# An opening that scales its rows first and adds their shift last

## What is computed

```python
mod = cond @ ada_w[l] + ada_b[l]                 # cond = silu(c)
sh1, sc1, g1, sh2, sc2, g2 = jnp.split(mod, 6, axis=-1)
h = modulate(rms_norm(x, norm_mix_g[l]), sh1, sc1)      # h * (1 + scale) + shift
proj = h @ w_in                                  # layer 0: q, k, v of two kinds of attention
# stick-breaking attention (8 heads) and sliding-window attention (8 heads), then
x = x + g1 * (o @ w_out)
h = modulate(rms_norm(x, norm_ffn_g[l]), sh2, sc2)
x = x + g2 * conv_ffn(h, ...)
# layer 1: the same around an HGRN2 recurrence; a last rms_norm closes
```

## Time and profile before

| | |
|---|---|
| Median of 3 runs | 1299.79 us (1299.79 to 1300.24) |
| Profiled execution, its own time | 1300.57 us |
| Span of the profiled execution | 1298.8 us |
| Mean granted TensorE clock | 0.997 |
| TensorE busy | 97% of the span |
| VectorE busy | 63% |
| ScalarE busy | 43% |
| GpSimd busy | 4% |

### The profile page before, as it was taken

One profiled execution on the slowest core, in us unless ns is written; L12 is line 12 of the kernel. 1 busy time (PEld: TensorE's weight loads), 2 busy tenths in 40 slices (PEclk: granted clock), 3 DMA queues, 4 the chain that ended last, 5 costly groups with the idle time before them and its releaser, 6 DMA issues.

```text
span 1298.8 us, 18991 instructions
## 1 busy us (share of the span) xinstructions
PE 1262.1 (97%) x7071; PEld 1021.7 (79%) x7071; DVE 818.4 (63%) x1191; ACT 554.8 (43%) x837; POOL 46.8 (4%) x92
## 2 busy tenths in 40 slices
PE   6999998999999999999999999999999999999997
PEld 5777777868888888878778888888688888888786
DVE  5776667676666666556787887776855555552423
ACT  7665556343333333121356655653433333331212
POOL 1000000000000000001000000001000000000000
PEclk9999999999999999999999999999999999999999
DMA  9644520535445454556513222226233333332232
GB/s 331 196 130 146 163 81 2 163 97 162 145 142 146 134 154 145 172 160 226 184 55 94 66 82 74 78 78 210 66 102 96 96 95 97 97 97 97 92 103 81
DMA packets 190074, 160.09 MB, mean 123 GB/s; under 512 B 5271, under 2 KB 163176, under 8 KB 190018
## 3 DMA queue, kind: packets, MB, share of 16 engines
q1 hardware_dynamic: 177696, 116.34, 29.7%
q0 software_dynamic: 11776, 42.29, 10.8%
q10 hardware_dynamic: 546, 0.69, 0.1%
HBM read 157.20 MB, written 2.10 MB: 123 GB/s over the span
## 4 chain that ended last, share of the span: by engine, by line
PE 88%; DVE 5%; SPq 2%; ACT 2%; issue 1%; DMA 1%; DVEq 0%; ACTq 0%
PE proj L1684 62%; PE z L1684 21%; PE obank L1684 3%; PE misc L1684 1%; SPq L512 1%; SPq L522 1%; DVE normed L1106 1%; DVE hT_lo L1112 1%; ACT w_hi L654 1%; DMA w_raw<-ab_w_in 1%; DVE w_lo L1068 0%; DVE xT L1491 0%; PE z L2244 0%; ACT hT_hi L686 0%; PE misc L1957 0%
## 5 line engine op out<-in xcount | busy, mean ns | idle before, releaser
L1684 PE MATMUL proj<-hT_hi,w_hi 128*128 128x512 f32 x1112 | 439.6, 396 | 1.1 <-ACT hT_hi L686 0.9
L1684 PE MATMUL proj<-hT_lo,w_hi 128*128 128x512 f32 x1112 | 434.6, 391 | 2.9 <-DVE hT_lo L1112 2.9
L1068 DVE TENSOR_TENSOR w_lo<-w_raw,w_hi 128x1024 fp32r<-128x1024 f32 x189 | 231.1, 1224 | 321.4 <-ACT w_hi L654 321.3
L1684 PE MATMUL proj<-hT_hi,w_lo 128*128 128x512 f32 x1112 | 433.2, 390 | 0.0
L654 ACT ACTIVATE w_hi<-w_raw 128x1024 fp32r<-128x1024 f32 x191 | 201.9, 1058 | 404.0 <-PE proj L1684 230.9
L1684 PEld LDWEIGHTS proj<-hT_lo,w_hi 128*128 128x128 f32 x1112 | 208.8, 188 | 52.4 <-DVE hT_lo L1112 9.3
L1684 PEld LDWEIGHTS proj<-hT_hi,w_hi 128*128 128x128 f32 x1112 | 208.8, 188 | 50.3 <-issue 8.7
L1684 PEld LDWEIGHTS proj<-hT_hi,w_lo 128*128 128x128 f32 x1112 | 208.7, 188 | 44.2
L1684 PE MATMUL z<-gated_hi,w_hi 128*128 (+1 forms) x264 | 103.6, 392 | 2.7 <-DVE xT L1491 2.7
L1684 PE MATMUL z<-gated_hi,w_lo 128*128 (+1 forms) x264 | 103.1, 390 | 0.0
L1684 PE MATMUL z<-gated_lo,w_hi 128*128 (+1 forms) x264 | 103.0, 390 | 0.0
(11 more groups left out here) (342 smaller groups left out, 1485.5 us busy)
## 6 DMA issues: line engine op xcount, KB each, us to landing
ada_raw<-ada_w POOLq DMA_DIRECT2D x80, 512.0 KB, 4.2
w_raw<-ffn_w_gate SPq DMA_DIRECT2D x44, 512.0 KB, 3.8
w_raw<-ffn_w_up SPq DMA_DIRECT2D x44, 512.0 KB, 3.8
w_raw<-ffn_w_down SPq DMA_DIRECT2D x44, 512.0 KB, 3.3
w_raw<-hg_w_in SPq DMA_DIRECT2D x32, 512.0 KB, 4.1
ada_first<-ada_w SPq DMA_DIRECT2D x16, 512.0 KB, 11.0
w_raw<-ab_w_in SPq DMA_DIRECT2D x14, 512.0 KB, 4.0
w_raw<-ab_w_out SPq DMA_DIRECT2D x8, 512.0 KB, 4.2
```

The lines of the kernel that those rows point to most:

```text
L1068: nc.vector.tensor_tensor(w_lo[:, slot, :], w_raw[:, slot, :], w_hi[:, slot, :].bitcast(F32), ALU.subtract).then_inc(lo_done, 1)
L1684: return nc.tensor.matmul(dst, weights_ap, moving, start=start, stop=stop, skip_group_check=True)
```

## The change

- The loads are cut anew: weights of four units in four pieces of two channel blocks each (`quad_load`), between them the scale weights in three pieces of 2, 2 and 4 blocks (`SCALES`), and last the shift weights. Two further units (`EARLY`) are loaded among the shift pieces.
- x is turned unscaled. The factor of each row is spread by TensorE over all partitions (`diag`, two banks), and `x_hat` = xT times that row, made by VectorE for blocks 0 and 1 and by GpSimd for blocks 2 to 7 (`hat`). VectorE copies blocks 0 to 3 of xT out of the banks, ScalarE the rest.
- The first two pieces of scale columns are made by TensorE alone, in small products of the raw weights with cond (`scale_products`); the third as before, by sums on VectorE.
- The blocks `hT_hi` and `hT_lo` carry the scale but not the shift. The four units, now SQ, SQ+1, SK, SK+1, run over these. Their missing part, the weights times the shift, is a column of each unit (`quad_bias_of`, 128 small products behind the shift sums) that is added when the units are copied out of the banks.
- Then the blocks are made again with the shift (`shifted_high` on ScalarE, `shifted_value` and `shifted_low` on VectorE), for all later units; the first of them (SV) waits for them one by one (`fix_lo`).
- GpSimd also makes three of the four low parts of these units' weights (`quad_split`) and those of the next two units (`early_split`).
- SV and WK become ordinary units, both ahead of "B" 0; "T" 0 goes behind it.

```diff
-QUAD = [SQ, SK, SV, WK]
+QUAD = [SQ, SQ + 1, SK, SK + 1]
 STEPS0 = [
-    ("Q", 0), ("A", 0), ("T", 0), ("u", SQ + 1), ("B", 0), ("u", SK + 1),
+    ("Q", 0), ("A", 0), ("u", SV), ("u", WK), ("B", 0), ("T", 0),
...
+EARLY = len(QUAD) + 2
+PIECES = 4
+SCALES = [(0, 2, 0), (1, 2, 2), (2, 4, 4)]
+X_BASE = 4
...
             quad_load(0)
-            first_ada(1)
+            scale_load(0)
             quad_load(1)
+            scale_load(1)
+            quad_load(2)
+            scale_load(2)
+            quad_load(3)
+            sp.wait_ge(xt_full, DC)
+            for k in range(4):
+                shift_load(k)
+            unit_load(4)
             sp.dma_start(table2, tables[:, 2 * P:9 * P]).then_inc(bands_in, 16)
-            for u in range(4, len(UNITS0)):
-                if u < 6:
-                    sp.wait_ge(quad_low, u - 1)
+            for k in range(4, DC):
+                shift_load(k)
+            unit_load(5)
...
+            def hat(dc):
+                if dc < X_BASE:
+                    pool.wait_ge(x_early, dc + 1)
+                else:
+                    pool.wait_ge(x_new, dc + 1 - X_BASE)
+                nc.gpsimd.tensor_tensor(x_hat(dc), xT[:, dc, :], x_rstd[:], ALU.mult).then_inc(hat_pool, 1)
+            def quad_split(c):
+                pool.wait_ge(hi_done, c + 1)
+                if c == 2:
+                    pool.wait_ge(misc_full, MISC_AT["scale1"] + 1)
+                nc.gpsimd.tensor_tensor(quad_lo[c], quad_raw[c], quad_hi[c].bitcast(F32), ALU.subtract
+                                        ).then_inc(quad_low, 1)
+            def early_split(u):
+                pool.wait_ge(hi_done, u + 1)
+                nc.gpsimd.tensor_tensor(w_lo[:, u % 2, :], w_raw[:, u % 2, :], w_hi[:, u % 2, :].bitcast(F32),
+                                        ALU.subtract).then_inc(early_low, 1)
+            pool.wait_ge(spread_done, 1)
+            for c in range(1, PIECES):
+                hat(2 * c)
+                hat(2 * c + 1)
+                quad_split(c)
+            for u in range(len(QUAD), EARLY):
+                early_split(u)
...
+            def first_high(dc):
+                if dc < 2:
+                    act.wait_ge(hat_first, dc + 1)
+                else:
+                    act.wait_ge(hat_pool, dc - 1)
+                act.wait_ge(first_mods, min(dc // 2, 2) + 1)
+                nc.scalar.activation(hT_hi[:, dc, :], x_hat(dc), ACT.Copy, scale=scale_g[:, 0, dc:dc + 1]
+                                     ).then_inc(h_hi, 1)
+            quad_high(0)
+            act.wait_ge(misc_full, MISC_AT["small"] + 1)
+            nc.scalar.activation(small[:].rearrange("p a n -> p (a n)"), misc[:, 0:4 * 96], ACT.Copy
+                                 ).then_inc(misc_free, 1)
+            act.wait_ge(spread_full, 2)
+            nc.scalar.activation(x_rstd[:], zb[2][:], ACT.Copy).then_inc(spread_done, 1)
+            x_rows(4)
+            first_high(0)
+            first_high(1)
+            x_rows(5)
+            x_rows(6)
+            x_rows(7)
+            quad_high(1)
+            first_high(2)
+            first_high(3)
+            quad_high(2)
+            first_high(4)
+            first_high(5)
+            quad_high(3)
+            first_high(6)
+            first_high(7)
+            split(4, 0)
             act.wait_ge(small_ready, 2)
             nc.scalar.activation(lower[:, 1, :], lower[:, 0, :], ACT.Exp).then_inc(lower_exp, 1)
+            act.wait_ge(bands_in, 16)
+            nc.scalar.activation(table_r[:], table2, ACT.Copy).then_inc(bands_ready, 1)
+            split(5, 1)
...
+            def scale_products(i):
+                _, n, dc = SCALES[i]
+                for k in range(DC):
+                    if i and k % 4 == 0:
+                        pe.wait_ge(scale_in[i][k // 4], 32)
+                    if not i and k % 2 == 0:
+                        pe.wait_ge(scale_in[i][k // 2], 16)
+                        if k:
+                            keep_clock(zb[3], 1)
+                    for c in range(n):
+                        for row in range(0, P, QUADRANT):
+                            last = mm(column_bank[f"scale{i}"][row:row + QUADRANT, c:c + 1],
+                                      scale_raw[i][:, k, c * P + row:c * P + row + QUADRANT], cond[:, 2, k:k + 1],
+                                      start=k == 0 and c == 0)
...
+            for dc in range(3):
+                x_rows(dc)
+            dve.wait_ge(x_root, 1)
+            for i in range(TB):
+                nc.vector.tensor_scalar(diag[:, i, :], ident, sumsq[:, 16 + i:17 + i], None, ALU.mult
+                                        ).then_inc(diag_ready, 1)
+            x_rows(3)
+            hat(0)
             dve.wait_ge(misc_free, MISC_AT["small"] + 1)
+            scale_columns(0)
+            hat(1)
+            dve.wait_ge(hi_done, 1)
+            nc.vector.tensor_tensor(quad_lo[0], quad_raw[0], quad_hi[0].bitcast(F32), ALU.subtract).then_inc(low_first, 1)
+            first_low(0)
+            first_low(1)
             nc.vector.tensor_tensor(lower[:, 0, :], gamma[0], gamma[1], ALU.subtract).then_inc(small_ready, 1)
-            quad_split(0)
-            first_columns(0)
-            first_low(0)
-            quad_split(1)
-            first_block(1, 0)
-            for dc in range(1, HALVES0):
+            scale_sums(0)
+            scale_sums(1)
+            scale_columns(1)
+            scale_sums(2)
+            scale_sums(3)
+            first_low(2)
+            scale_sums(4)
+            scale_sums(5)
+            first_low(3)
+            scale_sums(6)
+            scale_sums(7)
+            scale_columns(2)
+            for dc in range(4, DC):
                 first_low(dc)
-                first_block(1, dc)
-            for i in range(HALVES0, DC):
-                first_block(1, i)
-            quad_split(2)
-            first_columns(1)
-            first_low(HALVES0)
-            quad_split(3)
-            for dc in range(HALVES0 + 1, DC):
-                first_low(dc)
+                shift_sums(2 * dc - 8)
+                shift_sums(2 * dc - 7)
+            shift_columns()
+            dve.wait_ge(unit_mm, len(QUAD))
+            dve.wait_ge(misc_free, MISC_AT["shift"] + 1)
+            shifted_value(0)
+            bias_columns(0)
+            shifted_low(0)
+            bias_columns(1)
+            dve.wait_ge(misc_free, MISC_AT["bias1"] + 1)
+            nc.vector.tensor_scalar(q_sb[:, 1, :], quad_banks[1][:], HEAD ** -0.5, quad_bias[:, 2:3], ALU.mult, ALU.add
+                                    ).then_inc(quad_out[1], 1)
+            for dc in range(1, DC):
+                shifted_value(dc)
+                shifted_low(dc)
+                if dc == 3:
+                    nc.vector.tensor_scalar(k_sb[:, 1, :], quad_banks[3][:], quad_bias[:, 3:4], None, ALU.add
+                                            ).then_inc(quad_out[3], 1)
```

449 lines of the change are left out of this document (229 added, 220 removed).

## The result

The changed kernel takes 1326.22 us (median of 4 runs, 1325.04 to 1326.74), the kernel before, run beside it, 1300.01 (4 runs, 1299.79 to 1300.33). The ratio is 1.0199, with a 95% interval of 1.0187 to 1.0211. The sign was forecast, the size wasn't: 1305.3 was predicted, 1316 was the upper end.

The account below looks back on a forecast made before the run. VectorE's list ahead of B1 was taken as the bound: B1 4.5 us late plus 1.0 for a clock fall gives +5.5, 1305.3 us on the median. The 8-in-10 range was 1297 to 1316.

Parts of the forecast that it names:

- Step 1: Opening, up to the first matmul of the four units: it starts at 22.8 us, 4.3 earlier than before.
- Step 2: The four units: TensorE needs 48.4 us; VectorE's list beside it ends at 49.7, so TensorE waits 1.3 us.
- price for GpSimd's operation: GpSimd's two-input operations in the opening: 0.7 to 1.4 us for a block, 1.2 to 2.4 for a split.
- Rival 1: Opening, 17 to 45 us: GpSimd and VectorE take turns, B1 moves a further 4 to 12 us, 1315 total; chance 0.28.
- Step 3: Shift as a column, behind the shift sums: A0 (first logits) starts at 54.4 us, leaving 2.7 of the 4.3 gained.
- Step 4: Blocks remade with the shift, added VectorE work: soft_a of A0 comes at 66.9 us, 3.6 late.
- the 95% that was named as a sign: VectorE, from 50 to 85 us: busy for 95% or more if its list is the bound.
- Step 5: WK's copies, now behind A0 on VectorE: A1's soft_a at 84.4, B1 (second cumulative product) at 86.3, 4.5 us late.
- The clock behind the wait: TensorE, idle 5.4 us ahead of B1: its clock may fall afterwards, charged at 1.0 us.
- Rivals 2 and 3: VectorE's list before B1 short enough: faster, -3.0, 1296.8 us, chance 0.17; or half of that, no change, 1300, chance 0.13.

Follow-up runs that it names:

- e2: The changed kernel with all of GpSimd's arithmetic (six x_hat products, three lower parts, splits of units 4 and 5) moved to VectorE; 1320.19 us.
- e9: The changed kernel with only the two splits of units 4 and 5 moved from GpSimd to VectorE, behind the shift columns; 1324.99 us.
- e4: The changed kernel with the eight clear_queries memsets moved from ahead of A1's soft_a to behind A1's softplus; 1328.49 us.
- e7: e2 with the eight clear_queries memsets put directly ahead of A2's soft_a instead of ahead of A1's; 1315.19 us.
- e10: e7 with SyncE's loads of units 6 and 7 also held back until the bias products are done; 1314.77 us.
- e1: The kernel before with eight GpSimd operations on a spare buffer, released during VectorE's sums and copies; 1301.31 us in one run.
- e12: The kernel before with GpSimd operations on a spare buffer again, some while VectorE does nothing, others beside its sums or in idle time; 1302.80 us.

## Where the prediction was right and wrong

The difference of the profiled executions is 25.2 us, where 5.5 was forecast. The 19.7 between are 17.6 at A0 and 2.1 behind B1; from A0 to B1 nothing is off.

**Step 1, the first matmul: wrong by 2.9.** It started at 25.67, not 22.8, 1.4 us ahead of before. The fourth piece of x landed at 11.2 and not at the 9.5 that a spacing of 1.37 us gave: that spacing was read from other loads, in another stretch. The transposes began at 11.35, 1.9 us late. The list behind them took 10.3 us instead of 9.7, and from its end to the first matmul, with a wait of 2.96 us for ScalarE, it was 4.0 us instead of 3.6.

**Step 2, the four units and VectorE's list: this is the step that failed.** Its end was put at 49.7 and came at 63.94, 14.2 late: 2.9 from step 1, 10.1 from turns, 1.2 other. The other is the clock: it was 0.50 from 25 to 27 us and 0.58 from 27 to 29, and the 20 matmuls ahead of the second scale products took 6.1 us (25.67 to 31.73) instead of the 4.6 that 0.228 each gives. VectorE waited for those products, idle for 6.44 us until 33.04. The prediction took VectorE's sums and lows at the lengths that they have alone, so the wait of VectorE for GpSimd was put at nothing, and it found GpSimd's own duration indifferent "side by side with VectorE". That wait measured 10.1 us. e2 and e9 show that this was the term: without all overlaps the stretch is 7.8 us shorter, without the last two 4.05. Its price for GpSimd's operation was right for a block (1.27 us, 0.7 to 1.4 said) and too low for a split (2.66 to 2.71 where GpSimd lost nothing, 1.2 to 2.4 said), and in turns that price is what VectorE pays.

Rival 1 had the mechanism, and a chance of 0.28. Its size (a further 4 to 12, worked with 10) agrees with the 10.1 in part by luck: it counted six blocks and three splits in 17 to 45 us, and 4.05 of the 10.1 come from the splits of units 4 and 5 behind them, which it left out; those it counted cost 6.1. Its condition had no row to stand on, as it said: the trace of before has no such pair. But by the rival's own line "every sum and low of the opening reads two tensors in SBUF", so the condition was met in the whole list; the evidence against it, a sum beside GpSimd's issuing of a transfer, was of another kind, as was said there. The rival's 1315 was short because it stood on the rest of the forecast.

**Step 3, the shift as a column: wrong by 3.4.** From the last shift sum to A0 it took 8.1 us, not 4.7. The 128 tiny products were priced by the 64 records that took 0.71; 3.1 us of the difference are the two holes. Without them the products took 3.5 us, the later ones at a clock of 0.50, so the price per product (2.8 us for all) was about right; the holes were not in it. 64 records in one piece can't show it, 256 do.

**Step 4, the remade blocks: right behind A0.** From A0 to VectorE's soft_a of A0: 12.4 us, forecast 12.5. Ahead of A0 VectorE waited twice for bias columns, 2.60 and 2.64 us, where the prediction had 1.5 in all; so it was busy for 80% of 50 to 85 us and not for the 95% that was named as a sign.

**Step 5, the copies of WK: right.** From soft_a of A0 to that of A1: 17.45 us, forecast 17.5, and B1 1.94 behind it as before. From A0 to B1 31.8 us, forecast 31.9. e4 and e7 confirm why: taking 5.1 us from that list brings A1's soft_a 3.2 nearer, down to ScalarE's time. TensorE's idle time ahead of B1 is 3.02 us and not 5.4, since its logits took 4.63 us instead of 2.42, at a clock of 0.50.

**The clock behind the wait: the mechanism right, the size off by 2.1.** The prediction had 1.0 us. From 104 to 110 us the granted clock is 0.50, B1 takes 5.49 us (3.04 before), and from B1 to A2 it is 8.37 us instead of 5.28, 3.1 more.

**Rivals 2 and 3** fell with step 2: each needed a shorter list on VectorE.

What isn't explained is small: from the last head's soft_a to the end e2, e7 and e10 need 1.3 to 2.3 us more than before does, where the changed kernel needs 0.1 more.

Why is even e10 slower than before? Its A0 is at 63.85, 6.8 us behind before: ahead of A0 stands the bias stretch, 6.9 us from 56.91 with 3.0 us of holes, which before doesn't have. The next 4.2 us come between A0 and A1 (21.3 us, before 17.05), where the clock is 0.50 from 60 to 70 us and the logits take 4.6 us instead of 2.42. At A2 it stands 11.0 us behind (98.15 against 87.11).

## What to carry to other kernels

Before work goes from VectorE to GpSimd, look at what VectorE does in the same microseconds. If VectorE's operands were in SBUF, a GpSimd operation that reads SBUF held it up, here, for as much of its own length as was left (1.0 to 2.1 us each in the changed kernel; GpSimd needs 2.66 us for a split that VectorE does in 1.22). So such a move pays in stretches in which VectorE waits or reads PSUM. One GpSimd operation, the product with a constant, held VectorE up for less than its recorded length. When an order is moved, price the thing that stands behind the moved work in the same queue: eight memsets gained 3 us at one wait and lost them at the next (e4), and kept them at a place with idle time (e7). Long rows of tiny matmuls are not priced by a short row of them.

## What the hardware did that was not expected

- GpSimd's operation with two inputs of 1024 columns takes 2.66 to 2.71 us on separate tensors (the splits of the changed kernel) and 1.89 where both inputs and the output are the same tensor (e1, e12); 512 columns take 1.27 and 1.04.
- GpSimd never lost a turn by much: in the changed kernel its splits beside VectorE took 2.85 to 3.45 instead of 2.66, in e12 1.89 beside it and 1.89 alone. VectorE's 1.28 became 2.95. A copy on GpSimd (1.04 us) holds VectorE up as well, a memset doesn't, and a VectorE copy out of PSUM isn't held up.
- TensorE stood still, by the reading above for want of instructions, behind each 128 listed tiny products: 0.9 to 1.9 us with no data transfers beside it or few, 2.7 and 3.2 with two loads of 512 KB under way.
- A tiny product with 128 columns of weights costs 0.42 us at half clock, four with 32 columns each, whose results go to four different quarters of the partitions, 0.14 together.
